# A fused two-block layer: the second attention of block 1 over two key chunks per block of 16 columns by 8 rows, with its bias moved and masked in another way

## What is computed

```python
def neighborhood_attn(q, k, v, rpb):          # 8 heads of 64, S = 512 = 8 rows x 64 columns
    cols = jnp.arange(GRID_W)                                  # GRID_W = 64
    col_start = jnp.clip(cols - B_KW // 2, 0, GRID_W - B_KW)   # B_KW = 16
    col_idx = col_start[:, None] + jnp.arange(B_KW)[None, :]
    dc = col_idx - cols[:, None] + (B_KW - 1)
    def row(r):
        r0 = jnp.clip(r - kh // 2, 0, rows - kh)               # rows = kh = 8, so r0 = 0
        kn, vn = kr[:, :, col_idx], vr[:, :, col_idx]
        sc = jnp.einsum('bchd,brckhd->bhcrk', qr, kn).astype(jnp.float32) * scale
        dr = r0 + jnp.arange(kh) - r + (B_KH_MAX - 1)
        sc = sc + jnp.transpose(rpb_f[:, dr[:, None, None], dc[None, :, :]], (0, 2, 1, 3))[None]
        p = jax.nn.softmax(sc.reshape(b, h, GRID_W, kh * B_KW), axis=-1)
        return jnp.einsum('bhcrk,brckhd->bchd', p, vn)
```

## Time and profile before

| | us |
|---|---|
| median of 3 runs (lowest, highest) | 1589.89 (1589.53, 1590.97) |
| the profiled execution | 1592.57 |
| its span in the trace | 1590.8 |

### The profile page before, as it was taken

One profiled execution on the slowest core, in us unless ns is written; L12 is line 12 of the kernel. 1 busy time (PEld: TensorE's weight loads), 2 busy tenths in 40 slices (PEclk: granted clock), 3 DMA queues, 4 the chain that ended last, 5 costly groups with the idle time before them and its releaser, 6 DMA issues.

```text
span 1590.8 us, 19360 instructions
## 1 busy us (share of the span) xinstructions
PE 1538.7 (97%) x7440; PEld 1274.8 (80%) x7440; DVE 852.0 (54%) x1322; ACT 625.1 (39%) x927; POOL 382.2 (24%) x334
## 2 busy tenths in 40 slices
PE   6999999999999999999999899999999998999998
PEld 5887777888888888888888778888888777888886
DVE  4545665434443333434468787443447878644435
ACT  3324665332432332324434366332342446532332
POOL 2002563001200000000439343201024934321111
PEclk8997999999999999999999999999999999999999
DMA  6330112333233232232232000423223200133231
GB/s 140 122 105 16 51 48 65 91 95 106 93 102 106 80 106 96 90 105 92 80 100 80 27 1 22 139 81 104 82 90 100 80 27 1 54 106 106 80 106 54
DMA packets 134312, 128.36 MB, mean 81 GB/s; under 512 B 19671, under 2 KB 128471, under 8 KB 134231
## 3 DMA queue, kind: packets, MB, share of 16 engines
q1 hardware_dynamic: 133047, 127.19, 25.6%
q10 hardware_dynamic: 1184, 0.07, 0.1%
HBM read 125.12 MB, written 2.14 MB: 80 GB/s over the span
## 4 chain that ended last, share of the span: by engine, by line
PE 83%; DVE 10%; ACT 3%; issue 2%; DMA 1%; POOL 0%; ACTq 0%; DVEq 0%; POOLq 0%
PE G L1584 63%; PE S L1566 5%; PE G L1678 5%; PE G L1566 4%; PE T L1662 3%; DVE w L1048 2%; PE G L1738 2%; ACT w L776 1%; DVE ab L1066 1%; DVE sq L1186 1%; DVE hs L1472 1%; DVE v L1062 1%; DMA gains<-in_norm_mix 1%; DVE sq L1446 0%; ACT ab L826 0%
## 5 line engine op out<-in xcount | busy, mean ns | idle before, releaser
L1584 PE MATMUL G<-gx,w 128*128 128x512 f32 x2928 | 671.4, 390 | 3.0 <-DVE w L1048 3.0
L1584 PEld LDWEIGHTS G<-gx,w 128*128 128x128 f32 x2928 | 548.8, 188 | 119.9 <-DVE w L1048 3.9
L1048 DVE TENSOR_TENSOR w<-raw,w 128x2048 fp32r<-128x2048 f32 x112 | 262.1, 2340 | 211.3 <-ACT w L776 211.2
L776 ACT ACTIVATE w<-raw 128x2048 fp32r<-128x2048 f32 x112 | 211.6, 1890 | 139.3 <-PE G L1584 110.1
L1584 PE MATMUL G<-kvb,w 128*128 128x512 f32 x960 | 218.4, 389 | 0.0
L1584 PEld LDWEIGHTS G<-kvb,w 128*128 128x128 f32 x960 | 180.2, 188 | 37.4
L646 POOL TENSOR_TENSOR t<-t,rden 128x512 f32<-128x512 f32 (+2 forms) x128 | 122.6, 960 | 179.3 <-DVE rden L1192 179.0
L661 POOL TENSOR_TENSOR t<-sig 128x512 f32<-128x512 f32 x24 | 35.3, 1472 | 358.4 <-DVE sig L1257 358.4
L1319 DVE TENSOR_TENSOR x<-G,x 128x512 f32<-128x512 f32 x56 | 38.6, 689 | 115.3 <-PE G L1584 115.3
L838 ACT ACTIVATE t<-sq,nm 128x512 f32<-128x512 f32 (+2 forms) x128 | 87.0, 679 | 28.0 <-DVE nm L1186 27.4
L721 POOL TENSOR_TENSOR sumsq_f<-sumsq_f,sq_f 128x512 f32<-128x512 f32 x7 | 9.1, 1300 | 333.4 <-ACT sq_f L806 333.4
(11 more groups left out here) (207 smaller groups left out, 1890.6 us busy)
## 6 DMA issues: line engine op xcount, KB each, us to landing
raw<-in_w_in SPq DMA_DIRECT2D x98, 512.0 KB
raw<-in_w_up SPq DMA_DIRECT2D x32, 512.0 KB
raw<-in_w_down SPq DMA_DIRECT2D x32, 512.0 KB
raw<-in_w_out SPq DMA_DIRECT2D x24, 512.0 KB
raw<-in_w_attn_proj SPq DMA_DIRECT2D x8, 512.0 KB
raw<-in_w_fourier_proj SPq DMA_DIRECT2D x8, 512.0 KB
biasb<-bias_table SPq DMA_DIRECT2D x8, 448.0 KB, 3.5
xin<-in_x SPq DMA_DIRECT2D x2, 1024.0 KB, 6.7
```

What stands on the lines that cost most here:

```text
L776: nc.scalar.activation(K.w[:, j % 2, 0, 0:n], K.raw[:, j % 2, 0:n], ACT.Copy).then_inc(K.w_hi, 1)
L1048: nc.vector.tensor_tensor(K.w[:, s, 1, 0:n], K.raw[:, s, 0:n], K.w[:, s, 0, 0:n].bitcast(F32), ALU.subtract).then_inc(K.w_lo, 1)
L1584: mm = nc.tensor.matmul(b[:, :], w(p, k), x(q, k), start=(k == i == 0), stop=(k == kts - 1 and i == len(PASSES) - 1))
```

## The change

The queries of the second attention are no longer taken in rows of the grid but in blocks of 16 columns by 8 rows, which makes 128 again (`blocks`, `grid`). Such a block only sees 32 columns, the 16 of its own and 8 on either side. So the keys are stored shifted by 8 columns within their row (`in_places`, `HANG`), and a unit's keys are two blocks of 16 columns by 8 rows of them, 256 in all (`B_KEYS`, `blocks_of`): the moving operand of its 3 score matmuls is now read in runs of 16 columns. The values are stored in the same blocks, for which their tiles are made feature-major and turned (form `"turn"`, two `K.T` in turn). A pair of units touches three chunks, so `values` has 9 matmuls, and the piece of `K.pt` that one of two units doesn't see is zeroed (`clear_b`).

For the bias SP makes a second table in memory (`K.rows`, one transfer of 1920 runs of 32 elements), from which a head's bias is one transfer of 128x256 into one of two new buffers `K.rawb`. POOL writes from it and from the mask (three forms, `MASKS`) the three biases that a head's blocks need (`B_BIAS`) into `K.biasb`, 256 columns each. Those of heads 0 and 1 are written ahead of the first attention, those of head h + 1 behind the first three units of head h. The mask comes in three transfers and two memsets.

```diff
-BIAS_ROWS = 2 * KH - 2
+BLOCK = KW
+HANG = KW // 2
+WINDOW = 2 * BLOCK
+B_KEYS = (slice(0, 2), slice(1, 3), slice(2, 4), slice(3, None, -3))
+B_CHUNKS = ((0, 2), (1, 3), (1, 3), (2, 4))
+B_BIAS = (0, 1, 1, 2)
+MASKS = ((HANG, WINDOW, 3 * BLOCK, 0), (0, WINDOW, 2 * BLOCK, BLOCK - HANG), (0, WINDOW - HANG, 0, 3 * BLOCK - HANG))
...
-    tiles += [(7 + t // 2, t % 2, "tm", ("vb", t)) for t in range(HALF)]
+    tiles += [(7 + t // 2, t % 2, "turn", ("vb", t)) for t in range(HALF)]
...
-        return K.qb[:, part, t, :].rearrange("p (i c) -> p i c", c=P)[:, :, ::-1]
+        return blocks(K.qb[:, part, t, :])[:, ::-1, :, ::-1]
...
-    return K.vb[:, part, 2 * (t % 2):2 * (t % 2) + 2, (t // 2) * SCOL:(t // 2 + 1) * SCOL]
+    return K.vb[:, part, :, t * P:(t + 1) * P]
...
+def blocks(ap):
+    return ap.rearrange("p (b r c) -> p r b c", r=KH, c=BLOCK)
+def grid(ap):
+    return ap.rearrange("p (r b c) -> p r b c", r=KH, c=BLOCK)
+def blocks_of(ap):
+    return ap.rearrange("p (r b c) -> p b r c", r=KH, c=BLOCK)
+def in_places(to, t, g):
+    if to[0] == "kb":
+        t, g = [v.rearrange("p (r c) -> p r c", r=KH) for v in (t, g)]
+        return [(t[:, :, HANG:], g[:, :, :-HANG]), (t[:, :, 0:HANG], g[:, :, -HANG:])]
     if to[0] == "vb":
-        return ap.rearrange("p (t c) -> p t c", t=2)
-    return ap
+        rows = g.rearrange("p (r c) -> p r c", r=KH)
+        inner = rows[:, :, HANG:-HANG].rearrange("p r (b c) -> p r b c", c=BLOCK)
+        ends = g.rearrange("p (r u c) -> p r u c", r=KH, c=HANG)[:, :, ::1 - GRID_W // HANG]
+        return [(blocks(t)[:, :, 1:], inner), (t[:, 0:P].rearrange("p (r u c) -> p r u c", r=KH, c=HANG), ends)]
+    return [(t, g)]
...
-        lo, hi = (max(0, i - 1), min(TT, i + 2)) if self.kind == "A" else (0, TT)
+        lo, hi = {"A": (max(0, i - 1), min(TT, i + 2)), "B": B_CHUNKS[i], "L": (0, TT)}[self.kind]
...
-    sp.dma_start(K.mask[:, :], a["mask"]).then_inc(K.par_in, 16)
+    for v, (x0, x1, row, col) in enumerate(MASKS):
+        near = bass.AP(a["mask"].tensor, row * GRID_W + col, [[0, KH], [GRID_W, BLOCK], [1, x1 - x0]])
+        sp.dma_start(K.mask[:, v, x0:x1], near).then_inc(K.mask_in, 16)
...
-    for j in range(3, 9):
+    in_slab(3)
+    sp.wait_ge(K.tab_in, 16)
+    shifted = bass.AP(K.tab.tensor, TAB_PAD - HANG, [[1, BLOCK], [GRID_W, HEADS * (2 * KH - 1)], [1, WINDOW]])
+    sp.dma_start(K.rows.rearrange("(c r x) -> c r x", c=BLOCK, x=WINDOW), shifted).then_inc(K.rows_in, 16)
+    def bias_rows(h):
+        per = (2 * KH - 1) * WINDOW
+        src = bass.AP(K.rows.tensor, h * per, [[WINDOW, KH], [HEADS * per, BLOCK], [1, KH * WINDOW]])
+        sp.dma_start(K.rawb[h % 2][:, :, :], src).then_inc(K.biasb_in[h % 2], 16)
+    in_slab(4)
+    sp.wait_ge(K.rows_in, 16)
+    for h in range(2):
+        bias_rows(h)
+    for j in range(5, 9):
...
-    sp.wait_ge(K.tab_in, 16)
-    for h in range(HEADS):
-        if h >= 2:
-            sp.wait_ge(K.s_taken, S_B + TT * (h - 1))
-        start = TAB_PAD + h * TAB_H + GRID_W + KW - 1 - (P - 1)
-        src = bass.AP(K.tab.tensor, start, [[1, P], [1, BIAS_ROWS * GRID_W]])
-        sp.dma_start(K.biasb[:, h % 2, :], src).then_inc(K.biasb_in[h % 2], 16)
+    for h in range(2, HEADS):
+        sp.wait_ge(K.biasb_ok, 3 * (h - 1))
+        bias_rows(h)
...
-            if A.kind == "B" and n % TT == 0 and n // TT + 1 < HEADS:
-                masked(n // TT + 1)
             c = slice(A.first(), A.first() + (hi - lo) * P)
             pool.wait_ge(K.rden_ok, (A.u0 + n + 1).value())
             p = K.t[:, n % 3, c]
             nc.gpsimd.tensor_tensor(p, p, K.rden[:, n % 4:n % 4 + 1].broadcast_to([P, (hi - lo) * P]),
                                     ALU.mult).then_inc(K.probs_ok, 1)
-    def masked(h):
+            if A.kind == "B":
+                if n == 1:
+                    clear_b(0)
+                if n == 3:
+                    clear_b(1)
+                if n // TT + 1 >= 2 and n // TT + 1 < HEADS and n % TT < 3:
+                    masked(n // TT + 1, n % TT)
+    def clear_b(i):
+        pool.wait_ge(K.pv_done, HEADS * TT // 2 - 1 + i)
+        nc.gpsimd.memset(K.pt["B"][i][:, :, 3 * i, 1 - i, :].bitcast(F32), 0.0).then_inc(K.pt_zero, 1)
+    def masked(h, v):
         pool.wait_ge(K.biasb_in[h % 2], 16 * (h // 2 + 1))
-        b = K.biasb[:, h % 2, :].rearrange("p (r c) -> p r c", c=GRID_W)
-        nc.gpsimd.tensor_tensor(b, b, K.mask[:, :].unsqueeze(1).broadcast_to([P, BIAS_ROWS, GRID_W]),
+        if h >= 2:
+            pool.wait_ge(K.s_taken, S_B + TT * (h - 1))
+        raw = K.rawb[h % 2][:, :, :].rearrange("p r (o c) -> p o r c", c=BLOCK)
+        near = K.mask[:, v, :].rearrange("p (o c) -> p o c", c=BLOCK).unsqueeze(2).broadcast_to([P, 2, KH, BLOCK])
+        nc.gpsimd.tensor_tensor(K.biasb[:, h % 2, v, :].rearrange("p (o r c) -> p o r c", r=KH, c=BLOCK), raw, near,
                                 ALU.add).then_inc(K.biasb_ok, 1)
...
+    pool.wait_ge(K.mask_ok, 2)
+    pool.wait_ge(K.mask_in, 16 * len(MASKS))
+    for h in range(2):
+        for v in range(3):
+            masked(h, v)
     probabilities(Heads(K, "A"))
-    pool.wait_ge(K.par_in, 16 * PAR_DMAS)
-    masked(0)
...
+        places = zip(in_places(to, dst, psum(g)[:, :]), in_places(to, dst, K.rstd[:, :]))
+        for (dst, src), (_, rstd) in places:
+            if to[0] == "vb":
+                part = nc.vector.tensor_tensor(dst, src, rstd, ALU.mult)
+            else:
+                part = nc.vector.scalar_tensor_tensor(out=dst, in0=src, scalar=scale, in1=rstd, op0=ALU.mult, op1=ALU.mult)
+        part.then_inc(K.tile_out, 1)
...
-                dve.wait_ge(K.biasb_ok, h + 1)
-                off = (KH - 2 - 2 * i) * GRID_W
-                bias = K.biasb[:, h % 2, off:off + SEQ]
+                dve.wait_ge(K.biasb_ok, 3 * h + B_BIAS[i] + 1)
+                bias = K.biasb[:, h % 2, B_BIAS[i], :]
...
-                pairs = [(K.qb[r, p, t, qs], K.kb[r, q, t, :]) for p, q in PASSES]
+                keys = [blocks_of(K.kb[r, q, t, :])[:, B_KEYS[i]] for q in range(2)]
+                pairs = [(K.qb[r, p, t, qs], keys[q]) for p, q in PASSES]
...
-            product(K.S[(S + n) % 2][:, 0:w], pairs, K.s_full)
+            dst = K.S[(S + n) % 2][:, 0:w]
+            if A.kind == "B":
+                dst = dst.rearrange("p (o r c) -> p o r c", r=KH, c=BLOCK)
+            product(dst, pairs, K.s_full)
...
+            if A.kind == "B" and m < 2:
+                pe.wait_ge(K.pt_zero, 2 + m + 1)
             for i, k in enumerate(range(a0, b1)):
                 for p, q in PASSES:
-                    v = {"A": lambda: K.va[:, p, k, :], "B": lambda: K.vb[:, p, k, t * P:(t + 1) * P],
+                    v = {"A": lambda: K.va[:, p, k, :], "B": lambda: K.vb[:, p, (k + m % 2) % TT, t * P:(t + 1) * P],
...
+    def in_turn(k):
+        pe.wait_ge(K.tile_out, G_IN + k + 1)
+        late = [i for i in range(k) if IN_TILES[i][2] == "turn"]
+        if len(late) >= 2:
+            pe.wait_ge(K.split_lo, H_IN + late[-2] + 1)
+        for t in range(TT):
+            mm = nc.tensor.transpose(K.T[turns(k) % 2][:, t * P:(t + 1) * P], K.t[:, k % 3, t * P:(t + 1) * P], K.ident[:, :])
+        mm.then_inc(K.va_full, 1)
...
-        if form != "tm":
-            fm(g, wcol(Num(j), m), gx)
-        else:
-            b = bank(g)
-            w = K.w[:, j % 2, :, :].rearrange("p h (k c) -> p h k c", k=KT)
-            for i in range(2):
-                t = 2 * (to[1] % 2) + i
-                pairs = [(K.gx[:, p, kt, t * P:(t + 1) * P], w[:, q, kt, :]) for kt in range(KT) for p, q in PASSES]
-                product(b[:, i * SCOL:(i + 1) * SCOL], pairs, K.tile_full if i else None)
-        if k and IN_TILES[k - 1][2] == "turn":
-            pe.wait_ge(K.tile_out, g.value())
-            for t in range(TT):
-                mm = nc.tensor.transpose(K.T[0][:, t * P:(t + 1) * P], K.t[:, (k - 1) % 3, t * P:(t + 1) * P], K.ident[:, :])
-            mm.then_inc(K.va_full, 1)
+        fm(g, wcol(Num(j), m), gx)
+        if IN_TILES[k - 1][2] == "turn":
+            in_turn(k - 1)
+    in_turn(len(IN_TILES) - 1)
```

More of the change, by code:

```diff
@@ L82 @@
 KEY_SCALE = {5: 0, 6: 1}
-PAR_DMAS = 7 + LAYERS * 9
+PAR_DMAS = 6 + LAYERS * 9
 class Num:
@@ L233, in allocate @@
     K.big = K.kvb[:, :].rearrange("p (h t s) -> p h t s", h=2, t=KT)
-    K.mask = at("mask", 72, [P, GRID_W], F32)
+    K.mask = at("mask", 72, [P, 3, WINDOW], F32)
+    K.rawb = [at(f"rawb{i}", kb, [P, KH, WINDOW], F32) for i, kb in enumerate((72.5, 83))]
     K.biasa = at("biasa", 74, [P, 2, 3 * P], F32)
-    K.biasb = at("biasb", 77, [P, 2, BIAS_ROWS * GRID_W], F32)
+    K.biasb = at("biasb", 77, [P, 2, 3, KH * WINDOW], F32)
     K.sig1 = at("sig1", 74, [P, 4, SEQ], F32)
@@ L260, in allocate @@
     K.tab = nc.dram_tensor("bias_table", (TAB,), F32).ap()
+    K.rows = nc.dram_tensor("bias_rows", (BLOCK * HEADS * (2 * KH - 1) * WINDOW,), F32).ap()
     K.x_in = [semaphore(f"x_in{i}") for i in range(2)]
@@ L350, with turns @@
```

(23 more changed lines are left out.)

13 lines of the change are left out of this document (7 added, 6 removed).

## The result

| | us |
|---|---|
| before, median of 4 runs (lowest, highest) | 1589.71 (1589.03, 1590.97) |
| after, median of 4 runs (lowest, highest) | 1565.62 (1563.69, 1569.74) |
| ratio after / before, 95% interval | 0.9855 (0.9839 to 0.9871) |
| after, profiled execution (span) | 1563.69 (1561.8) |

Five further runs of the changed kernel on another chip gave 1566.19, ratio 0.9856 (0.9834 to 0.9878), against 1588.63.

What follows compares the result with a forecast made beforehand. The prediction took PE to bound the kernel, busy 97% of the span. 23.0 us gained in the second attention less 0.7 lost before the first made 22.3, from 1589.9 to 1567.6 us; eight in ten for 1562 to 1575.

Steps and rivals of the forecast that it cites:

- PE bounds the second attention, before and after: Second attention: PE's work sets the pace, a pair of units going from 4.41 to 2.91 us; 23.0 us gained.
- Its start and the clock: Second attention's start: first transposes at 192.5, about 1.2 earlier, then 13.1 us at half clock as before.
- My bounds (13.1 to 16.6): Second attention's half-clock part: taken at 13.1 us, up to 16.6 as in the first attention, leaving 21.5 us gained.
- The clock staying at full (10%, 1561.1): Rival, second attention's start: the clock doesn't fall, 13.1 us at half clock become 6.5 at full; 1561.1, 10%.
- The drain: End of the second attention: 0.5 us added because each unit waits for its own chain.
- POOL's operations: Second attention: bias operations at 0.87 us each, 2.5 us a pair of POOL, hidden behind PE.
- DVE and ACT keep the pace: Second attention: DVE and ACT stay under 2.5 us of PE's 2.91 a pair.
- the 3.1 or 3.3 of the rival: Rival, second attention: the round through DVE, ACT and POOL sets 3.1 or 3.3 us a pair; 1570.2 or 1572.6, 15%.
- The projection: Before the first attention: value tiles, turns and last tile take 26.0 us against 25.3; 0.7 us lost, between 0.4 and 1.1.
- SP's queue: Ahead of slab 3: two more mask transfers, slab 3 issued by 49.6 at the latest; hidden, little left at all bounds.
- The size of the whole: Whole kernel: 23.0 us gained less 0.7 lost, 22.3 us in sum.

Runs made afterwards that it cites:

- v12: The changed kernel with one chunk of the values multiplied twice in the second attention, 12 matmuls a pair and not 9: 1571.16 us, ratio 0.9887.
- t4: The changed kernel with two more transposes a unit in the second attention, whose results nobody reads: 1571.56 us, ratio 0.9887.
- s512: The changed kernel with second-attention scores over all 512 keys in plain order, of which the first 256 columns are used: 1575.03 us, ratio 0.9910.
- joined: The changed kernel with both attentions as one stream of 64 units, the second's first scores issued among the first's last units: 1559.02 us, ratio 0.9798.
- overlap2: overlap with the third score amid the last projection tile, the fourth behind it, and first transposes using the other K.T: 1550.12 us, ratio 0.9755.
- mask2b: The changed kernel with each of the three bias operations of heads 2 to 7 done twice, same output: 1570.38 us, ratio 0.9889.
- bulk: The changed kernel with a head's three bias operations in a row behind one unit, not spread over three: 1572.63 us, ratio 0.9883.
- overlap: The changed kernel with attentions in one stream, two scores ahead of the last projection tile, ACT's slab 9 split earlier: 1552.14 us, ratio 0.9770.

## Why the prediction was right, point by point

- **PE bounds the second attention, before and after.** Right: the chain holds nothing but PE pieces, and v12, t4 and s512 show each kind of piece to cost what its rows say.
- **Its start and the clock.** The transposes' start was met to 0.1 us and the half-clock part by the profiled execution, 13.7 for 13.1. That the second attention then gained 23.0 to the digit was in part luck: in the second profile of the same kernel the part was 6.8, and the second attention took 51.6 us, 25.8 less than before. My bounds (13.1 to 16.6) left out the low side. A part that stands at a fixed place need not have a fixed length. The clock staying at full (10%, 1561.1) happened in neither profile. Its price was also off: the pieces that I counted into the 13.1 us at half clock take 7.6 at full and not 6.5, by the same rows, so 5.5 us would have been saved and the rival stood at 1562.1. In the kernels whose clock stayed at full at a start, PE waited there for nothing (joined) or for 0.28 and 0.16 us (overlap2); in the changed kernel, with pauses of 0.96 and 1.08, it fell.
- **The drain.** 0.5 forecast, 0.5 measured.
- **POOL's operations.** Taken at 0.87, measured 0.74, the lower end. The mechanism is right: they stay hidden until POOL's sum passes PE's pair (mask2b) or three stand in a row (bulk). In the second attention DVE has a PSUM input in each large operation, and no bias operation took longer than 0.75. The Trainium skill, page "GPSIMD Engine Reference", section "Key points", has GpSimd contend with DVE instructions in a two-port mode or with two SBUF inputs. The trace agrees, as far as a case without such a DVE instruction can.
- **DVE and ACT keep the pace.** Right: 21.0 and 21.2 of 30.34 us, and a pair takes 2.91 us, not the 3.1 or 3.3 of the rival.
- **The projection.** 0.7 lost was forecast, 0.8 measured (60.18 to 129.00 before, 59.27 to 128.90 after), with another make-up than I worked out. This step was wrong, though the sum came out. The chain ahead of the first score:

```profile
120.62 1.92 ACT w L859
...
122.59 2.17 issue
124.77 0.75 DVE t L1169 x2
...
126.83 0.67 PE T L1837 x4
...
127.52 0.61 ACT kvb L903
...
128.15 0.70 DVE kvb L1145
...
128.90 2.94 PE S L1646 x9
```

ACT's split of slab 9 begins only at 120.62, since the high part of a turned tile, ahead of it on ACT, waits for the tile behind. So DVE's share of that split (122.56 to 124.85) lands in front of DVE's piece of the last tile but one (124.77), and the last tile's piece, whose matmuls end at 125.56, comes at 126.03. From those matmuls to the first score I had 3.3 us: the turn of the tile before (0.44), 2.2, the last turn (0.44) and 0.2. It took 3.3 too, but the turn of the tile before ran beside DVE's work and cost nothing, and in its place stood the 0.4 behind DVE's queue. I had costed the turns and the last tile, and not what queues behind ACT's wait; that the two errors cancelled was luck. Because of the same wait POOL's six bias operations came at 125.2 to 129.4 and not from 121.4 on, and were still ahead of the first probabilities at 132.78. overlap bears this out: with ACT's split moved ahead of that wait, DVE's share begins at 116.93 and its piece of the last tile but one at 120.06.
- **SP's queue.** Hidden, as said: slab 3 is issued at 45.42, 0.3 us later than before, since the three masks took 3.03 us together and not three times 2.23, and PE goes from the turn at 58.83 straight on to slab 3 at 59.27.

```profile
45.42 1.05 SPq L516 DMA_DIRECT2D raw<-in_w_in  x2
46.80 0.62 SPq L606 DMA_DIRECT2D bias_rows<-bias_table  x1
47.51 4.05 SPq L516 DMA_DIRECT2D raw<-in_w_in  x2
```

- **The size of the whole.** 22.3 forecast, 22.9 to 23 measured by the ratios. The profiled executions differ by 28.9, 6 us more; that goes with the clock outside of the second attention, whose three stretches make 6.7.

What stays open: what decides the length of a half-clock part, and which of the differences between overlap and overlap2 kept the clock up (shorter waits, or scores issued earlier). Only the profiled executions show where the parts lie, so whether overlap's faster runs had one at the first attention isn't known.
